# A decoder layer with dilated attention and retention: the mark at the attention stage's end, fewer halving adds, a split weight in two parts

## Time and profile before

| what | us |
|---|---|
| median of three runs (lowest, highest) | 854.59 (853.1, 855.23) |
| the profiled execution, own time | 854.84 |
| its span, first to last instruction | 853.1 |
| PE matmuls busy | 822.1 |
| DVE busy | 485.0 |
| POOL busy | 352.4 |
| ACT busy | 231.5 |

### The profile page before, as it was taken

One profiled execution on the slowest core, in us unless ns is written; L12 is line 12 of the kernel. 1 busy time (PEld: TensorE's weight loads), 2 busy tenths in 40 slices (PEclk: granted clock), 3 DMA queues, 4 the chain that ended last, 5 costly groups with the idle time before them and its releaser, 6 DMA issues.

```text
span 853.1 us, 19281 instructions
## 1 busy us (share of the span) xinstructions
PE 822.1 (96%) x7268; PEld 788.7 (92%) x7268; DVE 485.0 (57%) x839; ACT 231.5 (27%) x334; POOL 352.4 (41%) x261
## 2 busy tenths in 40 slices
PE   7999999999999999997898999999999999999996
PEld 6999999999999999997887888898899999999996
DVE  4367854787377854786454556555573333333467
ACT  5123421343032422440221321212162222222200
POOL 0069953898179934998520524215100000000003
PEclk8999999999999999999999999999999999999999
DMA  7998989769995989595939579396999888888942
GB/s 215 267 270 274 270 267 232 280 140 309 235 267 180 288 253 278 196 216 164 341 109 376 209 273 391 134 375 230 353 307 303 281 276 279 289 296 291 350 152 111
DMA packets 176203, 220.28 MB, mean 258 GB/s; under 512 B 9440, under 2 KB 153824, under 8 KB 174368
## 3 DMA queue, kind: packets, MB, share of 16 engines
q1 hardware_dynamic: 171072, 206.18, 77.2%
q0 software_dynamic: 4432, 11.15, 4.1%
q10 hardware_dynamic: 656, 2.36, 0.7%
HBM read 206.81 MB, written 100.14 MB: 360 GB/s over the span
## 4 chain that ended last, share of the span: by engine, by line
PE 64%; POOL 17%; DMA 7%; issue 6%; DVE 4%; SPq 1%; POOLq 0%; ACT 0%; DVEq 0%; ACTq 0%
PE bank L811 17%; PE bank L813 17%; PE bank L812 17%; POOL far L682 7%; DMA cslot<-in_cache_kv_w_dram 4%; PE bank L841 4%; PE bank L806 3%; POOL prod L682 2%; DMA out_dram<-st 2%; DVE wl L1515 1%; POOL far L685 1%; PE bank L936 1%; PE bank L1108 1%; PE bank L911 1%; POOL prod L685 1%
## 5 line engine op out<-in xcount | busy, mean ns | idle before, releaser
L811 PE MATMUL bank<-xh,wh 128*128 128x288 f32 x640 | 192.6, 301 | 0.1
L811 PE MATMUL bank<-wh,xh 128*128 128x256 f32 x640 | 185.1, 289 | 4.4 <-DVE qk L1742 4.1
L813 PE MATMUL bank<-xh,wl 128*128 128x288 f32 x640 | 189.0, 295 | 0.0
L812 PE MATMUL bank<-xl,wh 128*128 128x288 f32 x640 | 188.9, 295 | 0.0
L812 PE MATMUL bank<-wl,xh 128*128 128x256 f32 x640 | 180.0, 281 | 0.0
L813 PE MATMUL bank<-wh,xl 128*128 128x256 f32 x640 | 179.9, 281 | 0.0
L1515 DVE TENSOR_TENSOR wl<-raw,wh 128x1024 fp32r<-128x1024 f32 (+1 forms) x104 | 155.5, 1533 | 9.1 <-ACT wh L1320 8.3
L811 PEld LDWEIGHTS bank<-wh,xh 128*128 128x128 f32 x640 | 122.1, 191 | 8.6 <-DVE qk L1742 5.2
L682 POOL TENSOR_TENSOR far<-far,qrow 128x1024 f32<-128x1024 f32 x48 | 126.1, 2637 | 0.0
L1320 ACT ACTIVATE wh<-raw 128x1024 fp32r<-128x1024 f32 (+1 forms) x104 | 102.3, 1019 | 79.8 <-PE bank L841 40.9
L811 PEld LDWEIGHTS bank<-xh,wh 128*128 128x128 f32 x640 | 120.8, 189 | 1.9 <-DVE vn L1587 1.0
(11 more groups left out here) (214 smaller groups left out, 1507.9 us busy)
## 6 DMA issues: line engine op xcount, KB each, us to landing
raw<-in_w_in_dram SPq DMA_DIRECT2D x128, 256.0 KB
out_dram<-in_cache_kv_w_dram SPq DMA_DIRECT2D x32, 1020.0 KB, 10.2
cslot<-in_cache_kv_w_dram SPq DMA_DIRECT2D x24, 1024.0 KB, 8.7
out_dram<-in_cache_kv_w_dram SPq DMA_DIRECT2D x12, 2040.0 KB, 10.4
far<-in_cache_kv_w_dram SPq DMA_DIRECT2D x64, 256.0 KB, 7.0
out_dram<-in_cache_kv_w_dram SPq DMA_DIRECT2D x20, 504.0 KB, 8.6
far<-in_cache_kv_w_dram SPq DMA_DIRECT2D x16, 512.0 KB, 6.9
raw<-in_w_in_dram SPq DMA_DIRECT2D x16, 512.0 KB
```

Source lines behind the costliest of these rows:

```text
L811: pe.matmul(out, lhs[0](k), rhs[0](k), start=(k == 0), stop=False)
L812: pe.matmul(out, lhs[0](k), rhs[1](k), start=False, stop=False)
L813: last = pe.matmul(out, lhs[1](k), rhs[0](k), start=False, stop=(k == n - 1))
```

## The change

- `a_end` is counted up by two engines, ACT and DVE, and POOL, DVE, ACT and SP wait for 2. DVE waits ahead of its count for the stores of keys and values, for the first unit of stage B, and for the last sum. PE's one-column matmul and its two waits go, and so do POOL's count and its waits for the stores.
- DVE's three clears and its wait for `gn` stand behind its copy of unit 0.
- POOL adds halves in six pieces per head, 4 to 9, and no longer in 2, 3, 10 and 11; DVE sums those four over 128 elements.
- DVE's `low(c + 4, 0)` is in two: one half stands ahead of `queries(15, 2, 1)`, the other behind it. `far_sum(2)` stands behind `softmax(0)`, `far_sum(3)` behind `softmax(1)`.
- On PE, `turn_keys(0, 0)` stands ahead of `sample_values(0, 0)`.

```diff
--- before.py
+++ after.py
@@ -555,7 +555,7 @@
                     .then_inc(st_in, 16)
 
             retention_chunk(C0_B + 1, 0, 1)
-            sp.wait_ge(a_end, 4)
+            sp.wait_ge(a_end, 2)
             keys(0, 0)
             states(0)
             sp.wait_ge(far_out, H * 48)
@@ -690,8 +690,8 @@
                     m = k * FAR_PIECE
                     if k:
                         summed((0, 1, 3, 9)[k])
-                    product(prod[:, :, :], m, 0, k > 0)
-                    product(far[:, m:m + FAR_PIECE, :], m, 1, k > 0)
+                    product(prod[:, :, :], m, 0, k == 2)
+                    product(far[:, m:m + FAR_PIECE, :], m, 1, k == 2)
 
                 def distant(side):
                     pool.wait_ge(far_in[side], h * 128 + 128)
@@ -720,13 +720,10 @@
                 pool.dma_start(dst, fsum[:, 1, :]).then_inc(far_out, 16)
 
             with pool.Fori(0, H) as h:
-                own.enter(h, 10)
+                own.enter(h, 6)
                 cached_keys(h)
             own.leave(H)
-            pool.wait_ge(k_stored, H * 96)
-            pool.wait_ge(v_stored, H * 128)
-            pool.sem_inc(a_end, 1)
-            pool.wait_ge(a_end, 4)
+            pool.wait_ge(a_end, 2)
 
             own.after(pool.memset(qk[NS:P, QBLK, :], 0.0))
             own.after(pool.memset(half[:, :], -0.5))
@@ -1039,9 +1036,6 @@
 
             chunk_ready(C0_B)
             qk_unit(0, 0, 0)
-            for b in range(2):
-                pe.wait_ge(tg_free[b], TB_B + 1)
-            pe.matmul(bank[7][:, 0:1], ident, ident[:, 0:1], start=True, stop=True).then_inc(a_end, 1)
             for u in range(1, TT):
                 qk_unit(0, 0, u)
 
@@ -1260,8 +1254,8 @@
                 chunk_ready(r * B_CH + (n // B_UNITS * B_CH + C0_B + 1))
                 natural(1, r * B_UNITS + (n + U_B + 5 + 2), QBLK, 1)
 
+            turn_keys(0, 0)
             sample_values(0, 0)
-            turn_keys(0, 0)
             with pe.Fori(0, RH - 1) as r:
                 retention_head(r, False)
             retention_head(RH - 1, True)
@@ -1457,7 +1451,7 @@
                 else:
                     key_copy(r, 2)
 
-            act.wait_ge(a_end, 4)
+            act.wait_ge(a_end, 2)
             act.wait_ge(kd_done, 1)
             high(C0_B + 1, 1, lambda: act.wait_ge(unit_done, UD + U_B))
             act.wait_ge(cleared, 1)
@@ -1636,7 +1630,7 @@
                         m = FAR_M + x % 4 * FAR_PIECE
                         src = far[:, m:m + FAR_PIECE, :]
                         out = fsum[:, 1, x * FAR_PIECE:(x + 1) * FAR_PIECE]
-                    if 2 <= n < 12:
+                    if 4 <= n < 10:
                         src = src[:, :, 0:DH // 2]
                     dve.tensor_reduce(out, src, AX.X, ALU.add).then_inc(far_summed, 1)
 
@@ -1664,10 +1658,9 @@
                 far_sum(0)
                 far_sum(1)
                 queries(14, 2, 0)
-                low(c + 4, 0)
+                low(c + 4, 0, halves=(0,))
                 queries(15, 2, 1)
-                far_sum(2)
-                far_sum(3)
+                low(c + 4, 0, halves=(1,))
 
                 def za(n):
                     silu(16 + n, n, oa[:, bass.ds(h * NTOK + n * HALF, HALF)])
@@ -1680,8 +1673,10 @@
 
                 za(0)
                 softmax(0)
+                far_sum(2)
                 za(1)
                 softmax(1)
+                far_sum(3)
                 values(18)
                 far_sum(4)
                 far_sum(5)
@@ -1727,12 +1722,12 @@
             own.leave(H - 2)
             attention_head(H - 1, last=True)
             dve.wait_ge(tg_free[1], TB_B + 1)
+            dve.wait_ge(k_stored, H * 96)
+            dve.wait_ge(v_stored, H * 128)
+            dve.wait_ge(unit_done, UD + U_B + 1)
+            dve.wait_ge(far_summed, FAR_PIECES * (H + 1))
             dve.sem_inc(a_end, 1)
-            dve.wait_ge(a_end, 4)
-            dve.wait_ge(gn_in, 16)
-            dve.memset(qm[:, :], 0.0)
-            dve.memset(bank[4][:, :], 0.0)
-            dve.memset(pm[:, :], 0.0).then_inc(cleared, 1)
+            dve.wait_ge(a_end, 2)
 
             def projected(n, r, t):
 
@@ -1745,6 +1740,10 @@
                 tt(qk[0:NS, t, :], b[NS:P, 0:2 * RK], qk[0:NS, t, :], ALU.add).then_inc(unit_free, 1)
 
             projected(0, 0, 0)
+            dve.wait_ge(gn_in, 16)
+            dve.memset(qm[:, :], 0.0)
+            dve.memset(bank[4][:, :], 0.0)
+            dve.memset(pm[:, :], 0.0).then_inc(cleared, 1)
             low(C0_B + 1, 1)
             for t in range(1, TT):
                 projected(0, 0, t)
```

## The result

The changed kernel takes 877.01 us in the median of 20 runs, with single times from 853.15 to 885.99; the kernel before takes 853.27 (851.17 to 855.64, 20 runs). That is 2.8% slower by the medians, far outside the range of 846.5 to 853.3. Even of these three only one lies in the range. The profiled execution took 867.39 us, 865.7 of it span.

The account below looks back on a forecast made before the run. PE's matmuls, busy 96% of the span, were taken as the bound. Scores -3.0, stage end -3.4, clock +1.3 and joins -0.3 gave -5.4 us, from 854.84 to 849.4; range 846.5 to 853.3.

Parts of the forecast that it names:

- the part on the halving adds: Attention heads: POOL loses 2.6 us ahead of the value stores and 2.6 behind; DVE pays 2.1 us more per head.
- the rule: DVE instructions with two SBUF inputs and POOL ones reading SBUF exclude each other; a split loses up to 1 us: 849.8.
- DVE becomes the bound: Rival, 0.06: POOL comes no earlier, DVE's wider sums make each head's last gate product 2.1 us late; 860.3 us.
- The scores' wait is traded: Rival, 0.16: later split half or wide sums make PE wait at the value units, so 3.0 us comes back; 852.4.
- Scores: Term: with the split in halves, PE's wait for the attention queries' last copy goes in four heads; -3.0 us.
- Stage end: Term: the last sum of the last head comes earlier, so unit 3 of the next stage starts 3.4 us earlier.
- Clock: Term: the slow-clock stretch of some 3.4 us falls on unit 3 and what follows; +1.3 us, ends 0 and 1.7.
- the second wait grows: Rival, 0.09: unit 3 comes early, but the longer rotation wait draws its own slow stretch, another 1.7 us; 851.1.
- Joins: Term: one head's last gate product frees a bank for the next head 2 us earlier; 0.3 us gained, bounds 0 and 0.7.
- the turned keys: Term, start of retention: the 0.8 us wait for copied keys goes, the rotation wait grows equally; 0, other end -0.8.

Follow-up runs that it names:

- run 13: The changed kernel, but SP loads only half of the keys of pieces 12 to 15, the other half left out; 893.29 us, ratio 1.0458.
- run 1: The changed kernel, but POOL waits for the end of each unhalved product (pieces 0 to 3, 10 to 15) before issuing the next; 848.34 us, ratio 0.9930.
- run 11: The kernel before with only the weights' split in two around the last queries' copy and sums 2 and 3 behind the softmaxes; 853.31 us, ratio 1.0007.
- run 2: The changed kernel with the halving adds back in ten pieces, all else of the change kept; 858.57 us, ratio 1.0055.
- run 4: The changed kernel with the halving adds back in pieces 10 and 11 alone, eight pieces in all; 850.78 us, ratio 0.9957.
- Run 12: The kernel before with only the new end of the attention stage; 854.54 us, ratio 1.0028.
- run 6: run 1 with the keys turned behind the sample values, as before the change; 845.40 us, ratio 0.9912.
- run 5: The changed kernel with one wait of POOL for the end of its own product, behind piece 10 alone; 846.47 us, ratio 0.9929.
- run 8: run 1 with DVE's copies of units 1 and 2 ahead of its split of the values' weights; 841.93 us, ratio 0.9861.
- run 9: The changed kernel, but POOL waits for the last four pieces' keys ahead of pieces 10 and 11 instead of behind them; 847.20 us, ratio 0.9942.
- run 7: run 1 with 32 extra, unread matmuls on PE in its wait ahead of unit 3; 844.76 us, ratio 0.9912.

## Why the prediction was wrong

**The failed step** is in the part on the halving adds: "The split itself starts with POOL in an earlier product and ends some 0.8 us sooner", and in the price of the rule, "a split can lose up to 1 us more". I took each half to stand behind one POOL instruction, since the earlier trace rows showed that. But these rows are from a kernel in which every product near a split was followed by an add that waited for it, with a pause of 0.09 us between. The trace of before held the warning: the only unbroken runs were pieces 0 and 1 and the last four, and no split fell into them. In the changed kernel one half stood behind six products, 13.81 us, and PE waited 8.9. By run 13 that costs 9 us of waiting in each head in which it happens, and more through the clock: in run 13 from 103 to 118 us, with such a wait in it, the granted clock is 0.66 in the mean.

```profile
103.00:118.00 15.00, 6.41 (x29) 6.41 (x30) 13.73 (x13) 0.20 (x1) 4.78 (x3) 0.66 0.57 187
```

The Trainium skill ("SBUF — State Buffer", section "Who interferes with whom") says that the one that starts first holds the port pair for its whole instruction. The runs agree that such instructions exclude each other, and show more: a half of 1.22 us lasted 13.81 when six products followed each other closely, so the wait took in several whole instructions.

**The rivals.** "DVE becomes the bound", at 0.06, had the right engine, but the wrong mechanism, wider sums and a late POOL, and named `yb` where PE waited for `on`. In fact POOL was early, and that was part of the harm: it started piece 10 in the last head 1.3 us ahead of the split (380.97 and 382.25), where before it had started it 0.4 behind. In run 1, with the same sums, the last gate product waits 0.26 us for its sigmoid: DVE isn't the bound. "The scores' wait is traded" is what run 11 shows, but with POOL still halving in ten pieces.

**With the pauses back, the sum nearly held, in part by luck.** Run 1, which differs from the changed kernel only in the self-waits, takes 848.34 against 849.4, and is 4.6 us faster than the kernel before where 5.4 were forecast. Its terms, from its trace, which is of the slowest of its six executions (851.44):
- Scores: the wait is gone in all four heads, as forecast; but run 11 shows that the edit alone is worth 0.0. Run 2 still has the new waits for value and key rows and run 4 has not, so the gain needs the lighter POOL.
- Stage end: the last sum ends at 387.67 + 2.34 = 390.01, and ACT's rounding starts 4.80 later (4.79 forecast). From the turned outputs to unit 3 it is 398.65 - 385.68 = 12.97 against 408.96 - 392.57 = 16.39 before, so 3.4 earlier, the forecast term. That is a distance on PE; what it is worth in the time no run shows by itself.
- Clock: too small. I had 1.3 for one stretch of 3.4 us. Run 1's clock is at 0.50 from before unit 3 starts (398.65) to 404, and again at 418 to 421, behind the rotation's wait, so the case "the second wait grows" came on top. Half of these 5.4 and some 3.4 us is 4.4, an estimate from this trace. With it the sum gives 852.5 for an execution of 851.44. The mean clocks of run 1's six executions lie between 0.987 (the slowest, 851.4 us) and 0.994 (844.9), so most had less of it. That the median came out near 849.4 is luck as far as the clock goes. Run 12 alone gives +2.0 for the stage end with no gain against it. It is not most of run 2's 5 us: run 4 has the same stage end and is 2.2 us faster than the kernel before. PE's waits in run 2 add up to 12.5 us (6.8 for `qk`, 3.0 for the rotation, 2.7 for value and key rows) against 10.8, while the mean clock of the profiled execution is 0.986 against 0.992, which is 5 us of 859.
- Joins: 0.3, which no run shows by itself.

The lines of the stage end are, in run 1 and then in the kernel before:

```profile
394.81 2.00 ACT L1316 ACTIVATE wh<-raw 128x1024 fp32r<-128x1024 f32 x2 [8.52 <-POOL qdm L734]
```

```profile
385.68 0.60 PE L805 MATMUL bank<-con,on 128*128 128x128 f32 x4
...
398.65 0.58 PE L810 MATMUL bank<-wh,xh 128*128 128x256 f32 x1 [3.96 <-DVE qk L1739]
```

```profile
392.57 0.60 PE L806 MATMUL bank<-con,on 128*128 128x128 f32 x4
```

The last term, the turned keys: 0 was right or still too good (run 6).

**Left open**: why DVE's second half stands behind one product only after POOL has been held once, while POOL keeps DVE out before that (run 5). Where 4 of the 7.8 us between runs 2 and 4 come from. And whether the longer rotation wait draws the slow clock, which some traces show and others don't.

## What to carry to other kernels

An instruction that is taken out may have been the pause in which another engine got its turn: before you thin out one engine's work, look for what stands behind its back-to-back instructions, not only for how long each is. If a kernel's times spread where they did not before, look for a race between a landing and a queue, and force it to either side: one run each way shows both ends. And when a wait is closed, check what orders the next one; here two copies moved ahead of a split (run 8, 6.4 us against run 1 by the medians, 5.9 by the ratios) were worth more than all of the change with its pauses back (4.6).

## What the runs showed of the hardware

A DVE subtraction with two SBUF inputs took 1.22 us alone and 13.8 to 14.0 when it came into six unbroken POOL products of 2.33 us (the changed kernel and run 13); DVE's reductions with one SBUF input took 1.21 beside such products (run 9). One pause of less than 0.1 us between two POOL products (start to start 2.50 instead of 2.36) let it in (run 5) and made 30 us of difference to the kernel. Behind a PE wait of 3.9 to 4.0 us the granted clock was 0.50 for some 6.7 us in run 1 and 3.3 in run 5; with 32 matmuls in that wait (run 7) it stayed at 1.00.
